# The recurrence of an RWKV-7 layer: a 16-token part of each inverse moved to GpSimd, and the projections ahead of it merged with it

## What is computed

```python
xr, xw, xk, xv, xa, xg = (h + xx * mix[i] for i in range(6))
r, k, v = xr @ w_rkv[0], xk @ w_rkv[1], xv @ w_rkv[2]          # "wide" projections, 1024x1024
g = sigmoid(xg @ g1) @ g2                                       # low rank
for z in range(2):                                              # forward and backward
    decay = exp(-exp(wlog(w0[z] + tanh(xw @ w1[z]) @ w2[z])))   # low rank
    a     = sigmoid(a0[z] + (xa @ a1[z]) @ a2[z])               # low rank
    kz    = k * (1 + (a - 1) * k_a)
    ys.append(wkv_scan(r, decay, kz, v, -kk, kk * a, reverse=(z == 1)))

def step(state, inp):      # one token of one head, state is 64x64
    sa = state @ a_t
    state = state * w_t + outer(sa, b_t) + outer(v_t, k_t)
    return state, state @ r_t
```

## Time and profile before

| | us |
|---|---|
| median of 3 runs (4664.59 to 4670.62) | 4669.46 |
| the profiled execution's own time | 4669.28 |
| its span, first to last instruction | 4667.2 |
| projections, first to last matmul | about 2028 to 2250 |
| recurrence, first transposes to last matmul of the chain | 2294 to 2995 |

### The profile page before, as it was taken

How to read it: one execution, slowest core, us unless ns; L and a number is a source line. 1 busy time by engine, 2 the same in 40 slices (tenths; PEclk the granted TensorE clock), 3 DMA queues, 4 the chain that set the end, 5 groups by cost and what they waited for, 6 DMA issues and landing times. The chain is left out here.

```text
span 4667.2 us, 64270 instructions
## 1 busy us (share of the span) xinstructions
PE 4494.6 (96%) x24356; PEld 3595.2 (77%) x24356; DVE 2368.0 (51%) x4004; ACT 1475.6 (32%) x2066; POOL 303.3 (6%) x167
## 2 busy tenths in 40 slices
PE   6998999999999999999599999889999999999999
PEld 3465888888888888854499999758888888888887
DVE  5764875554245555540355655248755532444444
ACT  2252333333222222210443443223333332222222
POOL 0001340000000000000200000023400000000000
PEclk9999999999999999989899999999999999999999
DMA  6302245656566666522300000123456565555553
GB/s 249 131 1 81 95 138 192 206 200 213 168 227 234 215 234 236 180 104 101 141 31 22 24 20 20 46 82 113 141 188 217 192 205 168 205 194 192 195 190 131
DMA packets 248142, 690.92 MB, mean 148 GB/s; under 512 B 12920, under 2 KB 78712, under 8 KB 239904
## 3 DMA queue, kind: packets, MB, share of 16 engines
q1 hardware_dynamic: 240544, 654.99, 41.1%
q0 software_dynamic: 7424, 33.56, 1.9%
HBM read 533.27 MB, written 155.22 MB: 148 GB/s over the span
## 5 line engine op out<-in xcount | busy, mean ns | idle before, releaser
L1362 DVE TENSOR_TENSOR pe_lo<-pe_raw,pe_hi 128x2048 fp32r<-128x2048 f32 x222 | 508.9, 2292 | 1269.7 <-ACT pe_hi L1131 1269.7
L821 PE MATMUL bank<-pe_hh,pe_hi 128*128 128x512 f32 x2304 | 914.2, 397 | 37.5 <-POOL pe_lo L1235 37.4
L823 PE MATMUL bank<-pe_hh,pe_lo 128*128 128x512 f32 x2304 | 900.8, 391 | 0.0
L822 PE MATMUL bank<-pe_hl,pe_hi 128*128 128x512 f32 x2304 | 900.3, 391 | 0.0
L821 PE MATMUL bank<-pe_ah,pe_hi 128*128 128x512 f32 x2048 | 796.7, 389 | 0.0
L822 PE MATMUL bank<-pe_al,pe_hi 128*128 128x512 f32 x2048 | 796.7, 389 | 0.0
L823 PE MATMUL bank<-pe_ah,pe_lo 128*128 128x512 f32 x2048 | 796.7, 389 | 0.0
L1131 ACT ACTIVATE pe_hi<-pe_raw 128x2048 fp32r<-128x2048 f32 x272 | 520.4, 1913 | 587.1 <-PE bank L823 581.2
L821 PEld LDWEIGHTS bank<-pe_hh,pe_hi 128*128 128x128 f32 x2304 | 434.4, 189 | 126.0 <-POOL pe_lo L1235 39.6
L823 PEld LDWEIGHTS bank<-pe_hh,pe_lo 128*128 128x128 f32 x2304 | 434.0, 188 | 91.7
L822 PEld LDWEIGHTS bank<-pe_hl,pe_hi 128*128 128x128 f32 x2304 | 434.6, 189 | 85.9
(11 more groups left out here) (277 smaller groups left out, 5071.1 us busy)
## 6 DMA issues: line engine op xcount, KB each, us to landing
pe_raw<-in_stream SPq DMA_DIRECT2D x272, 1024.0 KB, 5.6
acts<-h SPq DMA_DIRECT2D x128, 512.0 KB, 6.9
gates<-pe_shared SPq DMA_DIRECT2D x32, 2048.0 KB, 7.4
pe_w<-gates SPq DMA_DIRECT2D x32, 2048.0 KB, 10.5
h<-acts SPq DMA_DIRECT2D x128, 512.0 KB, 4.1
ada_ring<-in_ada_w SPq DMA_DIRECT2D x32, 768.0 KB, 7.2
at_ada_ring<-in_ada_w POOLq DMA_DIRECT2D x16, 1024.0 KB, 7.6
rwkv_proj<-rp_out POOLq DMA_DIRECT2D x64, 256.0 KB, 2.7
```

The source lines that it names most:

```text
L821: nc.tensor.matmul(out, left[0], right[0], start=start, stop=False)
L822: nc.tensor.matmul(out, left[0], right[1], start=False, stop=False)
L823: return nc.tensor.matmul(out, left[1], right[0], start=False, stop=stop)
L1362: nc.vector.tensor_tensor(lo[:, side], raw[:, side], hi[:, side].bitcast(F32), ALU.subtract).then_inc(low, 1)
```

## The change

- `rwkv_project` becomes a class `Projections` whose parts are called inside the block of `rwkv_mix`, so there is no stage border between them. The wide projections become three float32r matmuls each (`split_matmul`: high by high, high by low, low by high), with the high parts of weights and inputs made by ScalarE, the low part of the weights by GpSimd and that of the inputs by VectorE. The narrow ones are spread between the wide ones of the first kind, and the last kind is v. `rp_xm` has one buffer. The stores move from GpSimd's queue to SP's. Chunk 0's loads and `front` parts are called while v is projected (from the output `V_AT` on).
- Levels 1 to 3 leave TensorE. In their place SP copies the 16-token diagonal blocks of `NT` (128 of them, 16 matrices by 8 blocks) through DRAM so that each lands on one partition, GpSimd inverts all 128 at once by elimination (15 steps of a multiply and an add, each waiting on the last), and SP copies the results back through DRAM into the diagonals of `Tm`, cleared before. Per chunk these are 8 + 2 + 2 + 8 DMAs.
- N itself is no longer made on TensorE; NT of chunk c+1 is made and copied out right after the levels of chunk c, and the relay and inversion for c+1 run while chunk c's chain and chunk c+1's transposes and products do. `double_p` of level 4 waits for `blocks_loaded`.
- `front` parts 0 and 1 of chunk c+2 move into chunk c's chain, one multiply (`key_part`) to GpSimd and one scaling (`scale_keys`) to ScalarE.

The core of the diff:

```diff
+    FIRST_LEVEL, NLEV = 4, LEVELS - 1
+    W = 1 << FIRST_LEVEL
+    NB = P // W
...
+                def relay(c):
+
+                    for z in range(2):
+                        sp.wait_ge(nt_out[z], 2 * c + 2)
+                    for b in range(NB):
+                        sp.dma_start(scratch("blocks", b), diagonal(NT, b)).then_inc(diag_stored, 16)
+                    sp.wait_ge(diag_stored, LANDED * c + LANDED)
+                    for z, dst in enumerate((packed_in, lower)):
+                        sp.dma_start(flat(half(dst, z)), scratch_half("blocks", z)).then_inc(packed, 16)
+                    sp.wait_ge(solved_done, c + 1)
+                    for z, src in enumerate((solved, turned)):
+                        sp.dma_start(scratch_half("inverses", z), flat(half(src, z))).then_inc(solved_stored, 16)
+                    sp.wait_ge(solved_stored, 32 * c + 32)
+                    sp.wait_ge(cleared, c + 1)
+                    for b in range(NB):
+                        sp.dma_start(diagonal(Tm, b), scratch("inverses", b)).then_inc(blocks_loaded, 16)
+
+                def body(c, side, further=True):
+                    if further:
+                        load_front(c + 2)
+                    relay(c + 1)
+                    if further:
+                        load_tail(c + 2, side)
...
+                def invert(c):
...
+                    then(gp.memset(solved[:, :, :], 0.0))
+                    settled()
+                    gp.wait_ge(packed, 32 * c + 32)
+                    then(gp.tensor_copy(half(lower, 0), half(packed_in, 0).rearrange("p i j -> p j i")))
+                    settled()
+                    then(gp.memset(flat(solved[:, :, :])[:, 0:W * W:W + 1], 1.0))
+                    for j in range(W - 1):
+                        settled()
+                        shape = [P, W - 1 - j, j + 1]
+                        part = outer[:, 0:(W - 1 - j) * (j + 1)].rearrange("p (i c) -> p i c", c=j + 1)
+                        then(nc.gpsimd.tensor_tensor(part, lower[:, j + 1:W, j:j + 1].to_broadcast(shape),
+                                                     solved[:, j:j + 1, 0:j + 1].to_broadcast(shape), ALU.mult))
+                        settled()
+                        then(nc.gpsimd.tensor_tensor(solved[:, j + 1:W, 0:j + 1], solved[:, j + 1:W, 0:j + 1], part,
+                                                     ALU.add))
+                    settled()
+                    gp.tensor_copy(half(turned, 1), half(solved, 1).rearrange("p i j -> p j i")).then_inc(solved_done, 1)
...
+                def body(c, side, first, last):
+                    if not last:
+                        key_part(c + 1, 1 - side)
+                        clear(c + 1)
+                        invert(c + 1)
...
-                    products("N", 0, A, B, side, n_done)
-                    products("NT", 0, B, A, side, nt_done, (tok_out, 5 * c + 1))
...
                     def double_p(lv, z):
-                        if lv > 1:
+                        if lv > FIRST_LEVEL:
...
-                            pe.wait_ge(prod_out, made + 9 + z)
+                            pe.wait_ge(prod_out, made + 5 + z)
+                            pe.wait_ge(blocks_loaded, LANDED * c + LANDED)
...
-                    for lv in range(1, NLEV + 1):
+                    for lv in range(FIRST_LEVEL, NLEV + 1):
                         double_p(lv, 0)
                         double_p(lv, 1)
...
+                    if not last_chunk:
+                        pe.wait_ge(bonus_out, c + 2)
+                        pe.wait_ge(ss_ready, c + 2)
+                        transposed_products(c + 1, 1 - side)
...
                         def without_u(z):
 
+                            if b == 0 and not last_chunk:
+                                pe.wait_ge(nt_out[1], 2 * c + 4)
```

and of the projections:

```diff
+        groups = [[(kind, c) for kind in range(3, 8)] for c in range(DC)]
+        self.outs = groups[0] + groups[1]
+        for m, wide in enumerate(self.WIDE):
+            self.at.append(len(self.outs))
+            self.outs.append(wide)
+            if m + 2 < DC:
+                self.outs += groups[m + 2]
...
+            if kind in (3, 5):
+                if n >= 3:
+                    pe.wait_ge(self.evacuated, n - 2)
+            elif kind not in (4, 6) and n >= 4:
+                pe.wait_ge(self.evacuated, n - 3)
...
+                m = self.wide_of(n)
+                pe.wait_ge(self.w_low, m + 1)
+                parts = self.parts[kind % 2]
+                for k in range(DC):
+                    if c == 0:
+                        pe.wait_ge(self.x_low, DC * kind + k + 1)
+                    last = split_matmul(nc, self.bank(n)[:, :], (self.wh[:, m % 2, k, :], self.wl[:, m % 2, k, :]),
+                                        (parts[:, 0, k, :], parts[:, 1, k, :]), k == 0, k == DC - 1)
+                last.then_inc(self.projected, 1)
...
+            m = self.wide_of(n)
+            if m is not None:
+                if m + 2 < len(self.WIDE):
+                    weights_high(m + 2)
+                if kind < 2 and c < DC // 2:
+                    for e in range(2):
+                        rows_high(kind + 1, 2 * c + e)
...
+                def first_sums(n):
+                    if n == V_AT + 2:
+                        sum_kk(0)
+                    if n == V_AT + 4:
+                        sum_bonus(0, 0)
```

More of the change, by code:

```diff
@@ L1512, in _ @@
                 mean_of_squares(K, pe, norm, 7, square)
-def rwkv_project(K, ada_acc):
-    nc, io = K.nc, K.io
+class Projections:
     WR, SR = 4, 4
     MIXES = (1, 4, 5, 0, 2, 3)
[L1524 to L1628, removed]
-                    bank = K.ps[(n + 3) % 4]
-                    if 3 <= kind < 7:
-                        bias = K.col("w0" if kind < 5 else "a0", (kind - 3) % 2 * DC + c)
-                        nc.scalar.activation(out[:, n % SR, :], bank[:, :], ACT.Sigmoid, bias=bias).then_inc(evacuated, 1)
-                    else:
-                        nc.scalar.activation(out[:, n % SR, :], bank[:, :], ACT.Copy).then_inc(evacuated, 1)
@@ L1980, in body, with parts, level @@
                                                           bank4(BANKS[i, z] + h)).then_inc(prod_out, 1)
-                    if not first:
-                        center(c - 1)
-                    for lv in range(1, NLEV + 1):
+                        if z == 0 and not first:
+                            rescale(c - 1)
+                    if first:
+                        for part in (0, 1):
+                            front(part, 1, 1)
+                    def parts(names):
+                        if not last:
+                            for part in names:
+                                front(part, c + 1, 1 - side)
+                    def level(lv):
                         for z in range(2):
@@ L1994, in body @@
                                                       ).then_inc(inv_out, 1)
[L1995 to L2001 removed]
+                    parts((4,))
+                    level(FIRST_LEVEL)
+                    if not first:
+                        gated_sum(c - 1, 1 - side)
+                    parts((3, 5))
+                    level(FIRST_LEVEL + 1)
+                    parts((8, 9, 6, 7))
+                    level(NLEV)
+                    if not last:
+                        copy_nt(c + 1)
                     for b in range(TC):
@@ L2130, in products, with transposed_products @@
                                 last.then_inc(sem_, 1)
+                def transposed_products(c, side):
+                    pe.wait_ge(factors, FACTORS * c + FACTORS)
+                    for z in range(2):
+                        products("NT", z, B, A, side, nt_done)
                 def body(c, side, first, last_chunk):
@@ L2287, in build @@
             K.end_stage()
[L2288 to L2289 removed]
+            stage_rwkv(K, across, shared)
         K.end_stage()
```

477 lines of the change are left out of this document (372 added, 105 removed).

## The result

| | before | after |
|---|---|---|
| median, us | 4669.21 (4664.59 to 4670.62, 4 runs) | 4440.04 (4436.77 to 4451.89, 4 runs) |
| ratio | | 0.9515, 95% interval 0.9496 to 0.9535 |
| span of the profiled execution | 4667.2 | 4435.4 |
| first level of chunk 0 | 2307.30 | 2261.97 |
| the same of chunk 7 | 2921.51 | 2716.64 |

The kernel is 229 us faster; 150 were forecast. The span is 231.8 shorter. It comes from the start of chunk 0 (45.3), seven chunks (614.2 - 454.7 = 159.5) and what is behind chunk 7's start (27.0). The forecast had 36.6, 89 and 24.3, so 70 of the 82 us that it missed in the span lie in the seven chunks.

The account below looks back on a forecast made before the run. TensorE, working without a break, bounds the recurrence. Savings of 36.6 at chunk 0's first level, 89 in seven chunks (75.0 against 87.7 each) and 24.3 for chunk 7, together 150 off 4669.3, give 4519; range 4430 to 4650.

Parts of the forecast that it names:

- The mechanism: Before level 4 of each chunk: the relay is only partly covered, so TensorE waits some 14 us.
- Rivals 1, 2 and 4: The fourth: casts, GpSimd's part or loads hold the projections' wide tiles, 36 lost, 4555; 0.12 together with the third.
- rival 1: Recurrence: relay hidden if at most 27.3 us; chunk 59.1, time 4392; chance 0.13, hidden or nearly so.
- L: Relay length in each chunk, from the copies of NT to the landing of the inverses: 41 us, between 24 and 68.
- rival 2: Recurrence: relay longer than what it replaces, kernel slower, from a relay of 59.8 us; chance 0.10.
- sweep of stores: Relay: eight stores of 256 64-byte pieces, 0.05 us a piece, 8.5 us; bounds 5.7 and 17.7.
- inversion: Relay: 34 GpSimd operations at a fixed 0.34 us each plus 3.7 for elements, 15 us; bounds 7 and 23.4.
- sweep of loads: Relay: eight loads of 64-byte pieces into the diagonals, 8.5 us, same bounds as the sweep of stores.
- queue term: Relay: wait behind the next chunk's input load on the same queue, 3 us, bounds 0 and 5.
- Rival 3: Inversion: GpSimd and VectorE hold each other up, relay grows by 8.7 us, time 4589; 0.12 together with the fourth.
- The rest of the chunk: Chunk without the relay: levels, sums and transposes 27.9, VectorE late 0.8, clock 2.2, NT's groups 1.9, copies 1.2.
- The projections: Before the recurrence: wide tiles 5.44 instead of 6.96 us, chunk 0's factors covered; end at 2221, where it was 2250.

Follow-up runs that it names:

- e8_unmerged: Against the changed kernel, chunk 0's input loads, factor work and two sums wait until the projections are stored; 4470.23 us.
- three last edits: Against the changed kernel: relay sweeps shared by SP's and GpSimd's queues, factor parts called earlier, TensorE's chunk loop written out; together 4406.78 us.

## Why the prediction was right in kind and 79 us short

**The mechanism held.** TensorE waits for the inverses in chunks 0, 1, 2, 4 and 6 (no relay, elimination twice), the relay sets the pace, a microsecond of it is worth eight to nine. Rivals 1, 2 and 4 fell, the first not by much: the relay is not hidden (no relay: 51 us less; rival 1's 59.1 for a chunk is what that kernel shows between turns, 59.06), but L is 32.7, nearer to its 27.3 than to my 41. It is far from rival 2's 59.8, and the projections are bound by TensorE. L came out near the low end of what I had allowed, 30 to 57, so the time lies in the range by a small margin.

**The step that failed is the size of L**, 41 in the forecast. Its terms, and what they are in chunk 1:

| term | forecast | measured |
|---|---|---|
| wait behind the next inputs' load | 3 | none that a row shows |
| sweep of stores | 8.5 | 5.0 |
| packed loads | 2.7 | 3.4 |
| inversion | 15 | 16.1 |
| stores of the inverses | 2.7 | 2.6 |
| sweep of loads | 8.5 | 5.5 |
| semaphores | 0.6 | in the above |
| sum | 41 | 32.6 |

The sweeps and the queue term are 9.5 too long and make more than the 8.4 us of difference; the packed loads and the inversion were too short. At 8 a microsecond the 8.4 are 67 of the 79.

The sweeps carried 6.5 of excess because I priced 256 pieces of 64 bytes by the engines' time, at 0.05 each. They are mostly the time of eight issues, 3.74, and what the last one still needs. My bound from below, 5.7, was above the truth, since I took the landing of a 256 KB store (2.7) for one of 16 KB. The page gives 2.0 and 2.2:

```profile
blocks<-x SPq DMA_DIRECT2D x64, 16.0 KB, 2.0
rm_T<-inverses SPq DMA_DIRECT2D x64, 16.0 KB, 2.2
```

The price of a piece can be read. The stretch of chunk 1's loads (length, busy of PE, PEld, DVE, ACT, POOL; clock, DMA share, GB/s):

```profile
2322.05:2327.57 5.52, 2.29 (x30) 1.91 (x30) 5.49 (x10) 0.67 (x1) 2.36 (x1) 0.85 0.23 24
```

24 GB/s in 5.52 us are the 128 KB of this sweep, so nothing else was moved. The 16 DMA engines were busy for 0.23 of the stretch, 1.3 us each for 128 pieces: 0.01 a piece, not 0.05. So the pieces don't bound the sweep. The shared sweeps halved the issues and gained at most 0.8 of a possible 1.9, so the issues are a part of it and not all.

The queue term was one for a collision that did not come. The 1.5 MB were on their way when the stores began (issued 4.4 before), and the sweep still took 5.0. Only in chunk 0, with 2 MB issued 1 us before, it took 9.3 (5.4 in `e8_unmerged`, where they were issued 5.3 before); there I had 6.5 + 8.5 = 15.

**Two errors cancelled in the inversion.** An operation's fixed part was 0.34 in the forecast; alone, the inversion takes 12.3, that is (12.3 - 3.7) / 34 = 0.25. And the sharing with VectorE costs 3.1 to 4.0. I charged nothing for it because I took the mean of a joined row for the time of each operation; read one by one, shows the hold. So 15 came near 16.1 by luck. Rival 3 was real, at less than half its 8.7: the two-input operations of VectorE's factor work, not its whole busy share, meet the inversion. The early factor parts took 2.2 of it away.

**The rest of the chunk** was 34.0 in the forecast (27.9 + 0.8 + 2.2 + 1.9 + 1.2) and 32.3 in the trace. The clock's 2.2 is 1.6 in the mean (30.6 without a wait), although the waits were a quarter of what I expected. It grows more slowly than they do: behind the waits of 9.3 to 16.6 with the elimination done twice it is 3.4 in the mean.

**The projections** end at 2223.3 (forecast 2221), and NT of chunk 0 follows without a gap. Both terms were confirmed, float32r (36) by a start of chunk 0 that comes 32.4 later without it, chunk 0's factors under v by one that comes 28.0 later. **Chunk 0's first level** came 8.7 earlier than forecast, by the sweeps. **Behind chunk 7's start** it is 27.0 for 24.3. Two sums of the prediction are slightly off, without effect: the upper bounds of L's terms make 69.8 and not 68, and its formula for a sweep gives 8.7 at 0.05 a piece and not 8.5.

What I overlooked is the turn of the loop, 7.5 us in chunks 3 and 5 without a relay. It was in the kernel before as well, with 2.8 of idle (TensorE's timeline of before, the transposes of two chunks):

```profile
2557.96 1.96 PE L2139 MATMUL bank<-consts,rm_B 128*128 128x128 f32 x8 [2.84 <-issue]
...
2735.53 1.97 PE L2139 MATMUL bank<-consts,rm_B 128*128 128x128 f32 x8 [2.81 <-issue]
```

Under a relay that is longer anyway it costs nothing, so the kernels with and without relay differ by less than the sum of the waits suggests.

Left open: why some of SP's issues take 0.5 to 1.3 us longer in some chunks and kernels, and when exactly the clock falls after a short wait. Which of the three last edits the 31 us need is open too: the written-out loop alone, and the shared sweeps with only one of the others, were not run.

## What to carry to other kernels

A chain of small dependent transfers costs its issues and its landings; price it by the landing of the smallest transfer at hand, not by pieces, and put the bound from below there. When one chain of steps sets the pace, test the repairs together as well: three edits that were worth 0 (one) and 5 us (the other two) were worth 31 together. Each of the smaller sets left waits with slow matmuls behind them, all three none from chunk 1 on. Before a row that joins operations is used as a price, look at its single operations: a mean can hide one that stood still. And ask which engine's two-input operations run while GpSimd is on the critical path.

## What was unexpected of the hardware

- A wait of 1.44 us was followed by matmuls at half clock (16 in 3.25 instead of 2.00, granted clock 0.57), and one of 1.72 was not (1.97, granted clock 1.00). The length of the last wait alone doesn't tell. In the first case TensorE had waited for VectorE 4 us earlier as well, 1.16; but after 1.11 and 3.15 in the same place the repeated run of the changed kernel had its 16 matmuls in 2.14 and the half clock only behind them.
- GpSimd's 39-element multiply took 0.25 alone and 1.05 beside a scan of VectorE. In the kernel before it was VectorE that stood still: 4.99 for an operation of 0.68, until GpSimd's had ended.
- A turn of TensorE's loop cost some 4.5 us of idle and 3 more in slow matmuls in the kernel without relay.
- The same eight issues on SP took 3.75 in one kernel and 4.9 to 5.1 in others whose SP code is the same.
